# A two-layer diffusion transformer on one core: output projection's weights loaded before the scan's last tile is done, input tiles scaled ahead of the modulation, and two weight tiles loaded ahead of the modulation matrix

## The reference, cut to what matters

```python
m = (jax.nn.silu(c) @ mod_w[layer] + mod_b[layer])[:, None, :]
sh_a, sc_a, ga, sh_f, sc_f, gf = jnp.split(m, 6, axis=-1)
h = rms_norm(x, g[0]) * (1.0 + sc_a) + sh_a        # the first norm, ahead of the input projection p = h @ w_in
...
out = ((yn + bonus).astype(v.dtype) * g) @ w_o     # rwkv_output: z = (yn + bonus) * g, then the projection
x = x + ga * rms_norm(y, g[1])
f = rms_norm(x, g[2]) * (1.0 + sc_f) + sh_f
x = x + gf * rms_norm(swiglu(f, ffn_w1[layer], ffn_w3[layer], ffn_w2[layer]), g[3])
```

## Time and profile before

| | us |
|---|---|
| median of 3 runs | 2573.28 (2570.63 to 2573.41) |
| profiled execution | 2573.34 |
| its span | 2571.5 |
| TensorE busy | 2311.7 (90%) |
| VectorE busy | 944.5 (37%) |
| ScalarE busy | 666.0 (26%) |
| GpSimd busy | 857.4 (33%) |

### The profile page before, as it was taken

The page is one execution under the profiler, slowest core; times in us unless marked ns, Lnnn a source line. Parts: engine busy times, 40 slices in busy tenths (PEclk is TensorE's granted clock), DMA queues, the critical chain, the costliest instruction groups (busy, mean ns, idle before and its releaser), DMA issues. The chain is left out here.

```text
span 2571.5 us, 50330 instructions
## 1 busy us (share of the span) xinstructions
PE 2311.7 (90%) x22240; PEld 1932.0 (75%) x22240; DVE 944.5 (37%) x1475; ACT 666.0 (26%) x1032; POOL 857.4 (33%) x699
## 2 busy tenths in 40 slices
PE   5899976998789999999939998999999867999997
PEld 3788854555489999999907987888888745888785
DVE  4110066792220000022378215677777523000123
ACT  4110065431230000112232133444444213111112
POOL 2133200100224344334205444333333223666562
PEclk8999988998889999999959999999999968999998
DMA  5655520001112212211202343222222121332221
GB/s 219 224 194 199 218 91 17 0 1 59 40 43 64 65 57 65 65 59 59 59 27 69 115 139 83 41 41 42 42 42 41 21 83 50 98 98 91 89 98 66
DMA packets 139266, 204.06 MB, mean 79 GB/s; under 512 B 87783, under 2 KB 97511, under 8 KB 131912
## 3 DMA queue, kind: packets, MB, share of 16 engines
q1 hardware_dynamic: 139080, 201.26, 24.7%
HBM read 183.93 MB, written 17.30 MB: 78 GB/s over the span
## 5 line engine op out<-in xcount | busy, mean ns | idle before, releaser
L258 POOL CAST TMP_r<-WR 128x1024 fp32r<-128x1024 f32 x120 | 126.9, 1058 | 749.9 <-DMA WR<-in_ffn_w_dram 438.0
L277 PE MATMUL PS<-H_r,TMP_r 128*128 128x384 f32 (+1 forms) x1088 | 331.4, 360 | 13.8 <-DVE Y_r L492 13.8
L277 PE MATMUL PS<-Y_r,TMP_r 128*128 128x384 f32 (+1 forms) x1088 | 330.6, 358 | 3.7 <-DVE H_r L492 3.7
L260 POOL TENSOR_TENSOR WR_r<-WR,TMP_r 128x1024 fp32r<-128x1024 f32 x120 | 290.0, 2417 | 9.6
L415 DVE TENSOR_TENSOR P<-TMP,PS 128x768 f32 (+1 forms) x44 | 36.1, 821 | 562.7 <-PE PS L277 562.7
L277 PEld LDWEIGHTS PS<-H_r,TMP_r 128*128 128x128 f32 x1088 | 202.2, 190 | 32.4 <-DVE Y_r L492 16.2
L277 PEld LDWEIGHTS PS<-Y_r,TMP_r 128*128 128x128 f32 x1088 | 202.0, 190 | 19.3 <-DVE H_r L492 4.0
L277 PE MATMUL PS<-H_r,WR_r 128*128 128x384 f32 x736 | 192.2, 343 | 0.0
L398 ACT ACTIVATE TMP<-PS 128x768 f32<-128x768 f32 (+1 forms) x44 | 31.0, 705 | 526.3 <-PE PS L277 526.3
L588 PE MATMUL PS<-H_r,TMP_r 128*128 128x384 f32 x704 | 151.9, 338 | 3.2 <-DVE H_r L626 2.2
L277 PE MATMUL PS<-Y_r,WR_r 128*128 128x512 f32 x352 | 139.3, 396 | 0.0
(11 more groups left out here) (314 smaller groups left out, 4534.4 us busy)
## 6 DMA issues: line engine op xcount, KB each, us to landing
WR<-in_ffn_w_dram SPq DMA_DIRECT2D x88, 512.0 KB, 3.5
TMP<-in_mod_w_dram SPq DMA_DIRECT2D x40, 1024.0 KB, 4.9
WR<-in_down_dram SPq DMA_DIRECT2D x44, 512.0 KB, 3.5
WR<-in_mix_w_in_dram SPq DMA_DIRECT2D x24, 512.0 KB, 6.8
WR<-in_rw_w_rkv_dram SPq DMA_DIRECT2D x24, 512.0 KB, 4.2
P<-in_mod_w_dram SPq DMA_DIRECT2D x4, 2048.0 KB, 21.6
vkr_dram<-extra SPq DMA_DIRECT2D x16, 384.0 KB, 4.8
scan_front<-vkr_dram SPq DMA_DIRECT2D x16, 384.0 KB, 4.1
```

Of the source, the lines that this page charges most:

```text
L258: nc.gpsimd.tensor_copy(hi, raw).then_inc(weights_hi, 1)
L260: nc.gpsimd.tensor_tensor(lo, raw, hi.bitcast(F32), ALU.subtract).then_inc(weights_split, 1)
L277: last = nc.tensor.matmul(PS[:, bank + b, 0:h1 - h0], w, x[:, h0:h1], start=k + p == 0, stop=k == CT - 1 and p == 2)
```

## The change

The edits in short:

1. `scan_sp` ends with a wait on "ys" of the last pair instead of z; the load of x back moves behind the loads of `mixout` (both groups), still after z.
2. YS and FIN move to EXTRA, EB and GTS to hyc.
3. In the last round ScalarE copies seven upper parts of z (behind "gt", after TensorE's "n_1"), VectorE subtracts them behind the last step of the chain of states; only the eighth stays behind z. TensorE does not wait for z as a whole any more, only for each input tile; ahead of weight tile 2 it waits for "gt" and "f1".
4. Two of the four first weight tiles are issued behind the tokens and ahead of the modulation matrix.
5. Norm 0 is scaled for all eight tiles straight into Y, ahead of the mod columns; ScalarE shifts in place.

```diff
@@ mixout_pe
             split_first_pe(pe, mixout, SPLITS["mixout"], SPLIT_MIXOUT)
+            pe.wait_ge(act_done, AC["gt", CT - 1])
+            pe.wait_ge(dve_done, DV["f1", CT - 1])
@@ norm_scale_dve (early: None, or the tile to scale into)
-            if between:
-                between()
             v.wait_ge(rstd_ready, q + 1)
...
-                if residual is None and t >= 2:
+                if residual is None and t >= 2 and not early:
                     v.wait_ge(normed, NORMED_BASE[q] + t - 1)
...
-                ins = nc.vector.tensor_tensor(flat(SCL[:, t % 2, 0:n]), flat(src(t)), rstd, ALU.mult)
+                dst = early(t) if early else SCL[:, t % 2, 0:n]
+                ins = nc.vector.tensor_tensor(flat(dst), flat(src(t)), rstd, ALU.mult)
                 ins.then_inc(scaled, 1)
-                if split and t:
+                if split and t and not early:
                     lower(t - 1)
...
+            if early:
+                between()
+                for t in range(CT - 1):
+                    lower(t)
@@ norm_shift_act
-                    last = nc.scalar.activation(dest(t, s0, s1), SCL[:, t % 2, s0:s1], ACT.Identity,
+                    raw = early(t) if early else SCL[:, t % 2, :]
+                    last = nc.scalar.activation(dest(t, s0, s1), raw[:, s0:s1], ACT.Identity,
@@ inputs_sp (behind the tokens, ahead of mod_w); inproj_sp
+            for t in range(2):
+                sp.dma_start(WR[:, t, 0:CT, :], inproj.w[t]).then_inc(w_full[t], 16)
...
-            for t in range(SLOTS):
+            for t in range(2, SLOTS):
@@ the views: YS, FIN, EB, GTS leave ARENA[5]
+        MK, RUN, YS, FIN = carve(EXTRA, [4 * TC, T, L, L])
+        EB, GTS = carve(hyc, [L, L])
@@ scan_sp, at its end
-            sp.wait_ge(dve_done, DV["z", CT - 1])
-            sp.dma_start(X[:, :, 0:L], x_keep).then_inc(x_back, 16)
+            sp.wait_ge(pe_done, PEM["ys", CT - 1])
@@ scan_act, behind "gt"
+                if i == CT - 1:
+                    act.wait_ge(pe_done, PEM["n_1", i])
+                    for k in range(CT - 1):
+                        nc.scalar.activation(ZH[:, k, :], Z[:, k, :], ACT.Copy).then_inc(input_hi, 1)
@@ scan_dve, behind steps(i, 10)
+                if i == CT - 1:
+                    for k in range(CT - 1):
+                        v.wait_ge(input_hi, SPLIT_MIXOUT + k + 1)
+                        nc.vector.tensor_tensor(ZL[:, k, :], Z[:, k, :], ZH[:, k, :].bitcast(F32), ALU.subtract)\
+                          .then_inc(input_split, 1)
@@ the blocks: sync
             dense_load(sp, mixout)
+            sp.wait_ge(dve_done, DV["z", CT - 1])
+            sp.dma_start(X[:, :, 0:L], x_keep).then_inc(x_back, 16)
@@ tensor
-            pe.wait_ge(dve_done, DV["z", CT - 1])
             mixout_pe(pe)
@@ scalar; vector
-            for k in range(CT):
-                act.wait_ge(dve_done, DV["z", CT - 1])
-                nc.scalar.activation(ZH[:, k, :], Z[:, k, :], ACT.Copy).then_inc(input_hi, 1)
+            act.wait_ge(dve_done, DV["z", CT - 1])
+            nc.scalar.activation(ZH[:, CT - 1, :], Z[:, CT - 1, :], ACT.Copy).then_inc(input_hi, 1)
...
```

More of the change, by code:

```diff
@@ L485, in norm_scale_dve @@
         def norm_scale_dve(v, q, src, n, residual=None, split=None, gains=0, between=None,
-                           each=None):
+                           each=None, early=None):
             def lower(t):
@@ L524, in norm_scale_dve, with norm_shift_act @@
                 each(CT - 1)
-        def norm_shift_act(act, q, n, l, k, dest, split=None):
+        def norm_shift_act(act, q, n, l, k, dest, split=None, early=None):
             def upper(t):
@@ L1896, in hybrid_dit_kernel @@
         TOKK, KINT, BVT, XY, OO, MT, NE = carve(ARENA[3], [2 * T, 2 * T, 2 * T, 4 * T, 4 * T, 2 * T, 2 * T])
-        KROOT, VROOT, KA1, W2S, A2S, BLK, YB, PROD, XB, LV, RSTEP, YS, FIN, EB, GTS, G2S, G2S2 = carve(
-            ARENA[5], [2 * NCH // 2, L // TC, CT, 128, 128, 512, 512, 512, 512, 4 * TC, 2 * L, L, L, L, L, 128, 128])
-        MK, RUN = carve(EXTRA, [4 * TC, T])
+        KROOT, VROOT, KA1, W2S, A2S, BLK, YB, PROD, XB, LV, RSTEP, G2S, G2S2 = carve(
+            ARENA[5], [2 * NCH // 2, L // TC, CT, 128, 128, 512, 512, 512, 512, 4 * TC, 2 * L, 128, 128])
+        MK, RUN, YS, FIN = carve(EXTRA, [4 * TC, T, L, L])
+        EB, GTS = carve(hyc, [L, L])
         Z = Yf[:, 0:CT * L].rearrange("p (c t) -> p c t", c=CT)
@@ L2956, in _ @@
             act.wait_ge(gains_ready, 1)
-            norm_shift_act(act, 0, T, 0, 0, lambda t, s0, s1: Y[:, t, s0:s1], SPLIT[0])
+            norm_shift_act(act, 0, T, 0, 0, lambda t, s0, s1: Y[:, t, s0:s1], SPLIT[0],
+                           early=lambda t: Y[:, t, :])
             inproj_act(act)
@@ L3016, in _ @@
             inputs_dve(v)
-            norm_scale_dve(v, 0, lambda t: X[:, t, :], T, split=SPLIT[0], between=lambda: mod_cols_dve(v, 0))
+            norm_scale_dve(v, 0, lambda t: X[:, t, :], T, split=SPLIT[0], between=lambda: mod_cols_dve(v, 0),
+                           early=lambda t: Y[:, t, :])
             for i in range(2):
@@ L3034, in _ @@
             scan_dve(v)
-            for k in range(CT):
-                v.wait_ge(input_hi, SPLIT_MIXOUT + k + 1)
-                nc.vector.tensor_tensor(ZL[:, k, :], Z[:, k, :], ZH[:, k, :].bitcast(F32), ALU.subtract)\
-                  .then_inc(input_split, 1)
+            v.wait_ge(input_hi, SPLIT_MIXOUT + CT)
+            nc.vector.tensor_tensor(ZL[:, CT - 1, :], Z[:, CT - 1, :], ZH[:, CT - 1, :].bitcast(F32), ALU.subtract)\
+              .then_inc(input_split, 1)
             v.wait_ge(x_back, 16)
```

## The result

The changed kernel takes 2554.15 us in the median (2544.86 to 2554.22, 5 runs) where the kernel before took 2573.28 beside it (2566.64 to 2574.31, 5 runs): a ratio of 0.9919, 95% interval 0.9897 to 0.9942, 19.1 us less. The forecast was 2554.3. The profiled execution took 2547.12 us, 7 less than the median.

What follows compares the result with a forecast made beforehand. TensorE was taken to wait at the scan's end for GpSimd's weight split and at the start for modulation; 2573.3 - 14.8 (tail) - 4.2 (start) = 2554.3 us, range 2549.5 to 2560.

Steps and rivals of the forecast that it cites:

- The tail: End of the scan: mixout's weights issued after "ys" instead of z release TensorE earlier, a gain of 14.8 us.
- The covers: End of the scan: idle ScalarE and VectorE time hides early copies and subtractions (4.8 us); x has 17 us of slack.
- The start: Start of the kernel: earlier scaling, less the delayed modulation matrix, ends TensorE's first pass sooner, a gain of 4.2 us.
- (b): Start: the DER operations are caught by GpSimd's L260, 2.6 later; pass ends at 66.4, a gain of 3.1 us.
- (a): Start: the DER operations slip through beside GpSimd's work; pass ends at 64.2, a gain of 5.3 us.
- take the middle, 4.2: Start: DER's arrival within 0.4 us of the deciding moment, so 4.2 us taken between gains of 5.3 and 3.1.
- part 2: Start: two input weight tiles ahead of the modulation matrix delay its last quarter, a loss of 2.4 us.
- part 3: Start: scaling before the modulation arrives leaves ScalarE 2.15 us per tile instead of 4.75; pass ends 5.3 or 3.1 earlier.
- The front gives nothing: Rival, start: late matrix, half-clock products and caught DER add to 6.9 us; gain 0 to 2; chance 0.15.
- The tail gives less: Rival, end of the scan: slower loads or GpSimd losing two more turns, 5 us, total 2559.3; chance 0.09.
- Full clock nearly from the start of the pass: Rival, both passes: TensorE at full speed early, 3.2 us more in front, 2 at the tail; 2549.1; chance 0.10.
- Slower: Rival, both passes: piecewise feeding keeps TensorE at half clock, 11.6 in front, up to 29 after; 2573.3 or more; chance 0.02.

Runs made afterwards that it cites:

- e1: Changed kernel with the start as before, so only the edits around the end of the scan; 2556.27 us, ratio 0.9936.
- e5: Changed kernel with mixout's weight loads issued only behind the last z, inputs still early; 2563.20 us, ratio 0.9967.
- e2: Changed kernel with all eight copies and subtractions behind z again, weights still early; 2553.63 us, ratio 0.9940.
- e11: Kernel before with only the start's edits: two weight tiles ahead of the modulation matrix and early scaling; 2565.27 us, ratio 0.9975.
- e10: Changed kernel run again, unchanged, for a second profile; 2553.95 us, ratio 0.9920.
- e6: Changed kernel with GpSimd waiting for the DER columns before it splits the third weight tile; 2548.32 us, ratio 0.9908.
- e3: Changed kernel with all four first weight tiles behind the modulation matrix again, early scaling kept; 2549.03 us, ratio 0.9910.
- e7: Changed kernel with all first weight tiles behind the modulation matrix, and mixout's weights issued earlier still, from "n_1" on; 2544.67 us, ratio 0.9902.
- e12: The kernel of e7 run again, unchanged, beside the changed kernel on one chip; 2545.56 us, ratio 0.9890.
- e8: Kernel before run again, unchanged, for a second profile; 2571.45 us, ratio 0.9999.
- e4: Changed kernel with scaling behind the modulation columns again, two weight tiles still ahead of the matrix; 2553.56 us, ratio 0.9922.

## Why the prediction was right

**The tail, 14.8 forecast.** Every step came where it was put. Issue 0.3 behind "ys" (0.2 forecast), first cast 4.3 behind it (3.8), TensorE released 11.5 behind it (11.4): the load took half a microsecond more than forecast, and the turn with VectorE cost GpSimd 0.3 instead of 0.7. z ended 12.0 behind "ys" (2.8 later than before, forecast 2.9), and the eighth input was ready at 2080.3, long before its row. 14.7 measured inside the profile, 15.5 by the time of e1. That the issue of the weights decides and not the inputs is shown by e5; that the inputs must be early too is shown by e2, where they become the wait that ends last. The covers held: seven subtractions took 4.29 for the 4.8 written down and cen did not wait for them; x came with 18 us to spare for the 17.

**The start, 4.2 forecast.** The pieces were right: matrix at 37.17 (36.6), products at full clock, third tile's cast at 39.64 (39.6), L260 at 40.76 (40.75). Case (b) happened, DER was caught by L260, and the pass ended at 66.86 (66.4); the third chunk came 2.75 earlier (case (b) had 3.1). In e11 case (a) happened: first L277 at 44.23 (44.15), pass over at 63.84 (64.2), 5.8 at the third chunk (5.3). One reading behind (a) was wrong: the 0.36 of the earlier trace rows was not DER beside a cast but DER waiting for the cast's end, as e5's 0.91 shows. It cost the forecast nothing, since the cast would be over at 40.7 by its own working. The weak step was to "take the middle, 4.2": neither case gives it. It did the sum no harm: of the five profiles with this start (after, e10, e2, e5, e11) four have the third chunk at 71.7 to 73.4, near (b), and one at 69.7, as in (a), and the medians give the start 3.6 (19.1 less e1's 15.5) or 7.8 (e11). A difference of 3 us between the two cases is below what they can tell. That the total came within 0.2 us of the forecast is luck: the executions of the changed kernel spread from 2537.72 to 2557.23, and only the agreement to a few microseconds, and the marks, speak for the working.

The Trainium skill ("SBUF — State Buffer", Who interferes with whom) has a VectorE operation with two SBUF inputs and a GpSimd operation that reads SBUF shut each other out for the whole instruction. The rows agree: 2.40 for DER behind L260 in the changed kernel, 0.24 with GpSimd held in e6, and 0.91 behind the start of a cast in e5. So the row of 0.36, which the prediction set against the rule, follows it too. What it leaves to the kernel is which of them comes first, and that was 0.04 us here and 0.24 the other way in e11.

**What the forecast missed.** It weighed part 2 only as a loss of 2.4 against the gain of part 3, and never asked for the sum without it. In the profiles without the early loads but with the early scaling (e3, e7, e12) the third chunk is used at 67.9 to 69.2, with both at 69.7 to 73.4: the change carries an edit that works against it, by 0.5 us in the best pair of profiles and by 2.5 or more in most. The working had the number (the delay of the matrix on the path that sets the start) but let the edit stand as given. It also gave the relay's 4.75 us without the condition on it, which is that GpSimd splits weights at the same time; e8 and e4 show what that condition does.

**The rivals.** "The front gives nothing" did not happen: with DER caught and the matrix late the gain was 2.75 all the same. The relay is gone, and GpSimd has fewer splits left that meet VectorE; e4, which keeps the relay and has DER end at the same time (43.25 for 43.20), still gains 1.5, so by these two profiles each accounts for about half. "The tail gives less" needed more lost turns; z lost one. The half clock that the first rival counts did occur: in e10, e2 and e5, which have the same start, the last products took 3.25 to 3.60. But the working added it to the caught DER, and e10 shows that the two overlap. Of the 6.9 us about 5.0 (2.4 + 2.6) could come, by the forecast's own terms. Full clock nearly from the start of the pass did not come: the last pair of 0.84 or so is at 52.04 and the first of 0.51 at 52.65, 5.3 us behind the first L277. "Slower" did not happen either: the pass left half clock sooner than before (5.3 us for 9.5), and the kernels with one part each, e1 and e11, are both faster.

**What stays open.** The profiled executions differ by 26.2 us and the medians by 19.1. 3.6 of the difference is there at the 7200th matmul, 14.6 arise in the mixout's first pass, and 5.9 lie in the scan, where the code is the same; e8 shows that this stretch can be as much shorter in the kernel before as well. Why it varies is not settled. The other 2 arise behind the pass and were not followed. And 23.3 (7.8 + 15.5) for the two parts alone against 19.1 for both lies inside the intervals (3.6 to 9.5, 12.6 to 20.3 and 14.9 to 26.5, by the ratios).

## What to carry to other kernels

A load that waits for the end of a computation should wait for the last reader of its buffer instead, and a bulk load with slack should queue behind it: the two gave 9.1 and 5.6 us here. Before loading something ahead of the transfer that everything waits for, price the delay (2.9 us for 1 MB between e3 and the changed kernel) against what the early tile is needed for; if its first reader waits for other data anyway, it is a loss. When a chain is judged, take a mark behind the place where its slack is swallowed (the third chunk, not the first matmul), and judge a few microseconds from the profile only where the stretch between two marks has been seen to repeat.

## What the runs showed of the hardware that was not expected

- Two VectorE operations of eight columns took 2.40 us when they came 0.04 us behind the start of a GpSimd subtraction of 2.34 (the changed kernel), 0.91 when they came 0.22 behind the start of a cast of 1.04 (e5), and 0.24 with GpSimd idle (e6).
- The sixteen products of the matrix's last quarter took 1.92 us in one execution of the kernel before and 3.25 in another (e8), at almost the same moment (34.19 and 34.07). The granted clock tells them apart: it was full (2.4 GHz) through the 1.92 of the kernel before and 0.58 of full through the 3.25, where it rose from half (1.2 GHz) on the way; e5's 3.60 stand at 0.53. Over the profiles the last quarter goes by turns with the third quarter, here in the kernel before and in e8:

```profile
28.90 3.57 PE L1526 MATMUL PS<-P,CS 128*32 128x512 f32 x16 [2.33 <-DMA P<-in_mod_w_dram]
```

```profile
28.79 1.92 PE L1526 MATMUL PS<-P,CS 128*32 128x512 f32 x16 [1.62 <-DMA P<-in_mod_w_dram]
```

In 12 of 13 profiles a last quarter of 1.92 or 1.93 follows a third of 3.38 to 3.64, with 1.6 to 1.9 us without work between them, and one of 2.95 to 3.60 follows a third of 1.92, with 3.4 to 3.7 between them; e2 is the exception (3.25 after 3.64 and 1.61). These are durations; for some of the early quarters, those of the changed kernel and of e2 among them, the trace has no reading of the clock. What decides the third quarter's clock is open.
- A stretch of the scan with the same instructions took 579.1 to 589.1 us in 13 executions. These 10 us are more than the start's edits are worth.
- Eight subtractions of 512 columns would take 4.29 / 7 x 8 = 4.9 without GpSimd beside them, by the seven of the changed kernel, and took 9.29 with it (e2).
